# A mixture of 32 experts, half of them narrowed to 64 rows and multiplied in plain float32 on two column halves of TensorE

## The reference

```
grp   = argmax(x @ w_group + b_group)                    # one of 4 groups per token
e1,e2 = top-2 of the 8 experts of that group
y     = w1 * expert(e1, x) + w2 * expert(e2, x)
expert(e, x) = (silu(x @ w_gate[e]) * (x @ w_up[e])) @ w_down[e]
```

## Time and profile before

| | |
|---|---|
| median of three runs | 1117.98 us |
| the profiled execution: own time, span | 1120.31 us, 1118.5 us |
| expert stage, first transpose of rows to the first instruction after down of the last | 497.2 to 1072.3 us |
| TensorE busy, share of the span | 98% |
| VectorE, ScalarE | 71%, 56% |
| moved by DMA | 288.3 MB |

### The profile page before, as it was taken

How to read it: one execution, slowest core, us unless ns; L and a number is a source line. 1 busy time by engine, 2 the same in 40 slices (tenths; PEclk the granted TensorE clock), 3 DMA queues, 4 the chain that set the end, 5 groups by cost and what they waited for, 6 DMA issues and landing times.

```text
span 1118.5 us, 15317 instructions
## 1 busy us (share of the span) xinstructions
PE 1090.7 (98%) x5369; PEld 901.1 (81%) x5369; DVE 799.0 (71%) x1127; ACT 626.6 (56%) x698; POOL 206.0 (18%) x187
## 2 busy tenths in 40 slices
PE   8999999999999999989999999999999999999976
PEld 7778899688887787868888888888888888888842
DVE  4220521245648787789999999998898989889787
ACT  5322231224336210247888887788888788888644
POOL 3001112000000000012343322233232332423200
PEclk9999999999999999989999999999999999999998
DMA  8622314811123321169999999999999999999784
GB/s 303 227 71 80 123 51 128 270 33 65 38 78 113 123 92 69 57 252 394 395 363 381 389 389 377 396 386 383 387 373 389 378 390 373 385 397 384 284 346 197
DMA packets 73369, 288.32 MB, mean 258 GB/s; under 512 B 16229, under 2 KB 24549, under 8 KB 47716
## 3 DMA queue, kind: packets, MB, share of 16 engines
q1 hardware_dynamic: 60320, 258.34, 60.8%
q0 software_dynamic: 11840, 25.09, 5.8%
q10 hardware_dynamic: 1156, 4.20, 0.9%
HBM read 266.66 MB, written 37.75 MB: 272 GB/s over the span
## 4 chain that ended last, share of the span: by engine, by line
PE 93%; DVE 3%; DMA 2%; issue 1%; ACT 1%; DVEq 0%; POOL 0%; POOLq 0%; ACTq 0%
PE bank L1651 26%; PE bank L1653 26%; PE bank L1652 26%; PE bank L1999 3%; PE bank L2099 2%; PE bank L2034 1%; PE bank L1837 1%; PE bank L1839 1%; PE bank L1886 1%; PE bank L1842 1%; DMA expert_rows<-yt,dix 1%; PE bank L1851 1%; PE bank L1797 1%; PE bank L1878 1%; PE bank L1729 1%
## 5 line engine op out<-in xcount | busy, mean ns | idle before, releaser
L1651 PE MATMUL bank<-whi,xghi 128*128 128x512 f32 x512 | 203.3, 397 | 1.0 <-DVE xglo L1495 1.0
L1653 PE MATMUL bank<-whi,xglo 128*128 128x512 f32 x512 | 200.4, 391 | 0.0
L1652 PE MATMUL bank<-wlo,xghi 128*128 128x512 f32 x512 | 199.9, 391 | 0.0
L1482 DVE TENSOR_TENSOR wlo<-raw_down,whi 128x2048 fp32r<-128x2048 f32 x64 | 146.2, 2292 | 27.8 <-ACT whi L825 27.7
L1651 PE MATMUL bank<-whi,xhi 128*128 128x512 f32 x384 | 155.2, 404 | 0.9 <-ACT num L768 0.6
L1653 PE MATMUL bank<-whi,xlo 128*128 128x512 f32 x384 | 151.3, 394 | 0.0
L1652 PE MATMUL bank<-wlo,xhi 128*128 128x512 f32 x384 | 151.0, 393 | 0.0
L1482 DVE TENSOR_TENSOR wlo<-raw,whi 128x2048 fp32r<-128x2048 f32 x64 | 146.4, 2288 | 4.2 <-ACT whi L825 3.2
L1482 DVE TENSOR_TENSOR wlo<-raw_up,whi 128x2048 fp32r<-128x2048 f32 x64 | 146.3, 2287 | 0.0
L825 ACT ACTIVATE whi<-raw_up 128x2048 fp32r<-128x2048 f32 x64 | 122.4, 1914 | 25.7 <-PE bank L1653 25.3
L825 ACT ACTIVATE whi<-raw_down 128x2048 fp32r<-128x2048 f32 x64 | 122.4, 1913 | 23.7 <-PE bank L1653 23.7
(11 more groups left out here) (341 smaller groups left out, 1708.9 us busy)
## 6 DMA issues: line engine op xcount, KB each, us to landing
raw<-l_w_gate SPq DMA_DIRECT2D x64, 1024.0 KB, 8.3
raw_up<-l_w_up SPq DMA_DIRECT2D x64, 1024.0 KB, 8.4
raw_down<-l_w_down SPq DMA_DIRECT2D x64, 1024.0 KB, 8.7
raw<-l_w_in SPq DMA_DIRECT2D x5, 2048.0 KB, 9.3
yy<-expert_rows SPq DMA_DIRECT2D x8, 1024.0 KB, 8.1
xt<-x_cols SPq DMA_DIRECT2D x8, 512.0 KB, 4.8
o_rows<-stage POOLq DMA_DIRECT2D x16, 256.0 KB, 3.2
qkT<-qk_rows SPq DMA_DIRECT2D x16, 256.0 KB, 3.7
```

The costliest lines, as they stand in the source:

```text
L1482: tt(wlo[k][:, halves(p)], raw_e[k][:, halves(p)], whi[k][:, halves(p)].bitcast(F32), ALU.subtract).then_inc(e_lo[k], 1)
L1651: t.matmul(out, lh, rh, start=first, stop=False)
L1652: t.matmul(out, lh, rl, start=False, stop=False)
L1653: return t.matmul(out, ll, rh, start=False, stop=last)
```

## The change

Experts are no longer taken in the order of their numbers. Experts 0 and 1 come first, as two with 128 rows ("large"). VectorE sorts the other 30 by their number of rows (`order`); the fifteen with most rows are large too, the other fifteen take 64 rows ("small"). Then come 15 pairs of one small and one large expert, and down of the last large one.

A small expert has its own buffers for weights, rows, hidden values and results. Its weights are used as loaded, with no `hi` and `lo`. Each chunk is two plain float32 matmuls with 64 stationary columns. One writes partitions 0 to 63 of bank 7 and the other 64 to 127: up and gate, or the two halves of down. That makes 16 matmuls for gate and up, 8 for down, and 12 transposes of 64 rows.

A large expert keeps its 72 matmuls and its 12 transposes. The low part of its weights is now written over the loaded weights, so a half of `raw_b` is free for its next load only when the matmuls on it are done. There is one `xghi` and `xglo` instead of two. An expert with more rows than its 64 or 128 would get a further pair; with these inputs there is none.

Further: some semaphores are merged (`wg_raw`, the gate biases, `hnw` and the meta tokens share one that waits for all four). The routing pieces move to pairs 1 to 5. The residual rows of all tiles are loaded before the last expert's end, where half of them were loaded after it.

The order on each engine in the expert stage:

```diff
@@ TensorE
+        def gate_up_small(s, p):
+            if p == 0:
+                pe.wait_ge(N["xs_cp"], s + 1)
+                wait(pe, N["y_s_cp"], s * 2)
+            wg, wu = [raw_s[k][:].rearrange("p (k n) -> p k n", k=KC) for k in range(2)]
+            pe.wait_ge(small_landed[0][p], s * 32 + 64)
+            for kk in range(4 * p, 4 * p + 4):
+                t.matmul(ps[7][0:SMALL, :], xT_s[:, kk, :], wu[:, kk, :], start=kk == 0, stop=kk == KC - 1)
+                last = t.matmul(ps[7][SMALL:, :], xT_s[:, kk, :], wg[:, kk, :], start=kk == 0, stop=kk == KC - 1)
+            last.then_inc(N["gu_s_mm"], 1)
...
+        def down_large(n, q):
+            pe.wait_ge(N["g_lo"], n + 1)
...
+                if q == 0 and k % 2 == 0:
+                    pe.wait_ge(e_lo[2], n * 2 + (k // 2 + 1))
...
+        def pair(i, ahead=1):
...
+            gate_up_small(i - 1, 0)
+            hidden_large(i)
+            gate_up_small(i - 1, 1)
...
+            rows_large(i + 1)
+            down_large(i, 0)
+            hidden_small(i - 1)
+            down_large(i, 1)
+            gate_large(i + 1)
...
+            down_small(i - 1)
             if ahead:
...
+                rows_small(i)
+            up_large(i + 1)
...
+        rows_large(0)
+        gate_large(0)
+        up_large(0)
+        rows_large(1)
+        hidden_large(0)
+        gate_large(1)
+        down_large(0, 0)
+        down_large(0, 1)
+        rows_small(0)
+        up_large(1)
@@ ScalarE
+        def pair(i, ahead=1):
+            silu_large(i)
+            hidden_hi(i)
+            hi_large(i, 2, 0)
+            silu_small(i - 1)
+            xg_hi(i + 1)
+            hi_large(i, 2, 1)
+            hi_large(i + 1, 0, 0)
+            hidden_small(i - 1)
+            y_large(i, 0)
+            hi_large(i + 1, 0, 1)
+            y_large(i, 1)
+            hi_large(i + 1, 1, 0)
+            y_small(i - 1)
             if ahead:
...
+                x_small(i)
+            hi_large(i + 1, 1, 1)
@@ VectorE
+        xg_lo(0)
+        order()
+        lo_large(0, 1, 1)
         for p in range(2):
...
+            lo_large(0, 2, p)
+        lo_large(1, 0, 0)
+        times_up(0)
+        lo_large(1, 0, 1)
+        xg_lo(1)
+        hidden_lo(0)
...
+        def pair(i):
+            times_up(i)
+            hidden_lo(i)
...
+            lo_large(i, 2, 0)
+            times_up_small(i - 1)
+            xg_lo(i + 1)
+            lo_large(i, 2, 1)
+            lo_large(i + 1, 0, 0)
...
+            lo_large(i + 1, 0, 1)
...
+            lo_large(i + 1, 1, 0)
+            lo_large(i + 1, 1, 1)
@@ SP, loads
+        def load_pair(i):
+            small = expert_at(i * 2)
+            for p in range(2):
+                for k in range(2):
+                    load_small(i - 1, small, k, p)
...
+                down_of(i)
+            large = expert_at(i * 2 + 1)
+            load_large(i + 1, large, 0)
+            for p in range(2):
+                load_small(i - 1, small, 2, p)
+            load_large(i + 1, large, 1)
```

More of the change, by code:

```diff
@@ L478, in _ @@
[L478 to L488, removed]
@@ L496, in _ @@
+        sp.wait_ge(N["ordered"], 1)
+        for i in range(1, 4):
+            load_pair(i)
+        sp.wait_ge(N["routed_n"], 1)
+        last_pair = sp.value_load(npm1[0:1, 0:1], min_val=PAIRS - 3, max_val=PAIRS - 3 + EXTRA) + 2
+        with sp.Fori(4, last_pair) as i:
+            load_pair(i)
+        load_pair(last_pair)
+        down_of(last_pair + 1)
+        sp.wait_ge(N["gu_s_mm"], last_pair * 2)
         for n in range(EARLY):
@@ L608, in scatter @@
[L608 to L616, removed]
@@ L619, in _, with gather_large @@
-        STATIC = 12
-        for s in range(2):
-            pool.sem_inc(tix_ready[s], STATIC + 2)
+        def gather_large(n, column=None):
+            wait(pool, N["xgT_mm"], n * 2)
+            if isinstance(n, int) and n < FIRST:
+                rows = tokrow[:, n:n + 1]
+            else:
+                if isinstance(n, int) and n == FIRST:
+                    g.memset(xg_b[:], 0.0)
+                rows = tix_b[:]
+                pool.wait_ge(gathered_b, n * 16)
+                g.tensor_copy(rows, tokrow[:, bass.ds(column, 1)]).then_inc(tix_b_ready, 1)
+                pool.wait_ge(tix_b_ready, n - (FIRST - 1))
+                pool.sem_inc(N["wait_passed"], 1)
+            g.indirect_dma_start(xg_b[:], None, h1_dram[0:T, :], bass.IndirectOffsetOnAxis(rows.bitcast(U32), 0),
+                                 bounds_check=last_token, oob_is_err=False).then_inc(gathered_b, 16)
@@ L827, in xg_hi, with hi_large @@
-        def xg_hi(j, b):
+        def hi_large(n, k, p):
+            if isinstance(n, int) and n == 1:
+                act.wait_ge(small_landed[k // 2][p], (32, 16)[k // 2])
+                act.wait_ge((N["g_mm"], N["u2_mm"], N["y2_mm"])[k], (p + 1, p + 1, p + 2)[k])
+                src = raw_s[k]
+            else:
+                act.wait_ge(ex_landed[k][p], 16 if isinstance(n, int) and n == 0 else n * 16)
+                src = raw_b[k]
+            a.activation(whi[k][:, halves(p)], src[:, halves(p)], ACT.Copy).then_inc(e_hi[k], 1)
@@ L852, in _, with y_small @@
+        def y_small(s):
+            wait(act, scattered_s, s * 16)
+            act.wait_ge(N["y_s_mm"], s * 2 + 2)
+            for q in range(2):
+                a.activation(yt_s[:, q * 512:(q + 1) * 512], ps[7][q * SMALL:(q + 1) * SMALL, :], ACT.Copy).then_inc(N["y_s_cp"], 1)
         for i in range(NT - 1):
@@ L869, in _ @@
         a.activation(r_s[:, 1, :], r_s[:, 0, :], ACT.Exp).then_inc(N["w_exp"], 1)
-        xg_hi(0, 0)
+        xg_hi(0)
         a.activation(ftmp[:, 0:1], ones[:, 0:1], ACT.Silu)
-        hi_expert(0, 2, 1)
-        hi_expert(1, 0, 0)
-        xg_hi(1, 1)
-        hi_expert(1, 0, 1)
-        silu(0)
+        hi_large(0, 2, 1)
+        hi_large(1, 0, 0)
+        silu_large(0)
+        hi_large(1, 0, 1)
+        xg_hi(1)
+        hidden_hi(0)
+        hi_large(1, 1, 0)
+        hi_large(1, 1, 1)
+        y_large(0, 0)
+        y_large(0, 1)
+        x_small(0)
         def scale_rows(tiles):
@@ new lines, in _ @@
+        for i in range(1, 4):
+            pair(i)
+        act.wait_ge(N["routed_n"], 1)
+        last_pair = act.value_load(npm1[0:1, 0:1], min_val=PAIRS - 3, max_val=PAIRS - 3 + EXTRA) + 2
+        with act.Fori(4, last_pair) as i:
+            pair(i)
+        pair(last_pair, ahead=0)
+        last = last_pair + 1
+        silu_large(last)
+        hi_large(last, 2, 0)
+        hidden_hi(last)
+        hi_large(last, 2, 1)
+        scale_rows((0, 1, 2))
+        a.activation(diags[:, 0, :], ident[:], ACT.Copy, scale=ALPHA).then_inc(N["f_scaled"], 1)
@@ L927, in squares @@
+        weight_diagonals((4,))
+        y_large(last, 0)
+        scale_rows((3,))
+        y_large(last, 1)
         def squares(n):
@@ L1566, in expert_sum @@
+        for i in range(1, STATIC):
+            pair(i)
+        dve.wait_ge(N["routed_n"], 1)
+        last_pair = dve.value_load(npm1[0:1, 0:1], min_val=PAIRS - 3, max_val=PAIRS - 3 + EXTRA) + 2
+        with dve.Fori(STATIC, last_pair) as i:
+            pair(i)
+        pair(last_pair)
+        last = last_pair + 1
+        times_up(last)
+        lo_large(last, 2, 0)
+        hidden_lo(last)
+        lo_large(last, 2, 1)
+        last_tokens(last)
         def expert_sum(n):
@@ L2051, in item @@
[L2051 to L2067 removed]
+            wl = lo_b[2][:].rearrange("p (k n) -> p k n", k=FC)
@@ new lines, in hidden_small, with down_small @@
+        def hidden_small(s):
+            pe.wait_ge(N["gu_s_done"], s + 1)
+            pe.sem_inc(N["wait_passed"], 1)
+            gv = gu_s[:].rearrange("p (m k) -> p k m", k=FC)
+            for k in range(FC):
+                last = t.transpose(ps[4][:, k * SMALL:(k + 1) * SMALL], gv[:, k, :], ident[0:SMALL, 0:SMALL])
+            last.then_inc(N["hT_s_mm"], 1)
+        def down_small(s):
+            pe.wait_ge(N["hT_s_cp"], s + 1)
+            wd = raw_s[2][:].rearrange("p (k n) -> p k n", k=FC)
+            for k in range(FC):
+                if k % 2 == 0:
+                    pe.wait_ge(small_landed[1][k // 2], s * 16 + 32)
+                t.matmul(ps[7][0:SMALL, :], hT_s[:, k, :], wd[:, k, 0:512], start=k == 0, stop=k == FC - 1)
+                last = t.matmul(ps[7][SMALL:, :], hT_s[:, k, :], wd[:, k, 512:], start=k == 0, stop=k == FC - 1)
+                if k % 2:
+                    last.then_inc(N["y_s_mm"], 1)
```

704 lines of the change are left out of this document (378 added, 326 removed).

## The result

The changed kernel takes 1210.32 us (median of 4 runs, 1207.23 to 1212.96), the kernel before 1117.31 in the same comparison: 1.0826 times as long, 95% interval 1.0802 to 1.0851. That is 93 us slower, where the forecast was 1173 (56 slower, range 1075 to 1215). The direction and the range held. The size did not: 37 us are missing from the sum, and the time lies above the 1145 to 1200 that the prediction gave as its likeliest rival's own range. The profiled execution took 1212.96 us, its span 1211.2.

The account below looks back on a forecast made before the run. TensorE bounds, with loads at 92% of their limit. Start 38.6, fifteen pairs of 38.7, routing 3 and end 8.7 make 630.8 us against 575.1, 55.7 more: 1173 us, range 1075 to 1215.

Parts of the forecast that it names:

- its likeliest rival: Small experts' matmuls on both column halves run together, with waits in each pair: 1173 us, own range 1145 to 1200, chance 0.67.
- the routing: Routing pieces moved to pairs 1 to 5, where VectorE is part of the chain: 0 to 8 us, taken as 3.
- the end: From the end of the last up, the last expert's hidden and down take 8.7 us, as before.
- Work of a pair: TensorE's work in a pair: 17.8 large expert, 10.3 small expert's matmuls, 1.2 its transposes; 29.3 us.
- Waits: TensorE's idle time in a pair, for copies and low parts on the other engines: 7.7 us together.
- Down's 4.4: Wait in the large expert's down: its second half's high part stands on ScalarE behind the next rows' copy; 4.4 us.
- up's 2.9: Wait in the next large expert's up: its second half's high part stands behind the small expert's copies; 2.9 us.
- gate's 0.4: Wait in gate of a pair: its second half comes 0.4 us late behind the copy of a large expert's result.
- The clock: TensorE's half-clock stretches after a pair's two waits: up to 3.4 us of work lost, taken as 1.7.
- the partial rival: The column halves overlap only partly, a small expert's matmuls cost 13 us: 40 more, 1213 us, chance 0.05.
- One after the other: The column halves don't overlap, a small expert costs 20.6 us and a pair 49.0: 154 more, 1328 us, chance 0.15.
- Loads become the bound: Faster rival: ScalarE and VectorE run ahead, so loads set the pair at 32.7 us: 1084 us, chance 0.13.

Follow-up runs that it names:

- the run with fewer bytes: The reordered kernel, reading only an eighth of each half of the small experts' down weights: 1056.3 us.
- the two runs that change one order each: Changed kernel with down's high and low parts made earlier: 1115.0 us; changed kernel with the high part of up's second half copied earlier: 1157.7 us.
- The smallest edit: Changed kernel with down's wait for a result copy-out made smaller by one, to the same half of the expert before: 1175.0 us.
- The filled waits: Changed kernel with order and waits kept, but TensorE multiplying the identity by itself into a free bank while it waits: 1163.3 us.
- the run on one half: Changed kernel with small experts' gate and up, and down's two halves, on the same column half, into two different banks: 1352.1 us.
- the reordered kernel: Changed kernel with the weaker copy-out wait, down's parts earlier (also for the last expert) and up's second half earlier: 1095.5 us.

## Why the prediction held, and by which terms it was too small

**The sum.** Measured on the same marks as in the forecast, the start of the stage took 537.05 - 497.43 = 39.6 us (forecast 38.6), the pairs 1158.2 - 537.05 = 621.2 (580.5 and 3 for the routing), the end 1170.18 - 1158.2 = 12.0 (8.7). From there to the end of the span it is 41.0, against 46.2 before: the tail gained 5.2 where I took 0. Off by 1.0, 37.7, 3.3 and -5.2, together the missing 37. Nearly all is the pair: 41.2 instead of 38.7, fifteen times. Of these 2.5 us, 1.7 are work, 1.4 are clock, and the waits took 0.7 off: two terms too small and one too large.

**Work of a pair.** Forecast 29.3, measured 31.0 by the run with fewer bytes: 25 us in fifteen pairs, the largest miss of the sum. The choice that the halves run together was right: a two takes 0.86. The yield of 1.59 that I estimated from the Trainium skill (TensorE: Matmul & The Clock Gate, Part 3) would have been 13.0 us for a small expert's matmuls; three blocks of 3.59 are 10.8, against 20.6 one by one. What was mis-sized are the transposes and the changes from one kind of instruction to another, about 0.1 each. The large expert's four transposes took 0.39 from start to start before (728.95 to 729.34) and take 0.68 now in front of plain float32 matmuls. In the pair of 31.00 us the small blocks took 10.75 where the sum held 10.3, the large expert's 72 matmuls 17.0 for 16.6, and the transposes 3.2 (0.68 and 0.90 for the large expert's, 0.62 and 1.03 for the small one's, from start to start) for 2.4.

**Waits.** Forecast 7.7, measured 6.4 idle and about 0.6 at their edges: the last matmul before a wait runs 0.40 where its slot is 0.23, and the first one behind it takes 0.33. Down's 4.4 was 3.2, up's 2.9 was 2.2, and gate's 0.4 did not come. Their places and their causes were as said, and the two runs that change one order each show it. For one wait the sum has no term at all: 1.05 before down's second half. `y_cp >= 2n + 1` is the copy-out of the first half of the same expert, and that copy stands on ScalarE behind `hidden_small`. The smallest edit removes it.

**The clock.** I took 1.7 a pair, half of the 3.4 that two full slow stretches could cost, because part of a stretch might lie in the wait. The filled waits put it at 3.1, 21 us more in fifteen pairs. In the pair shown both stretches come after the wait, in working time.

**The start, the routing, the end.** The first three pairs took 42.2 (from 540.64 three of them to 667.37) and the next eleven 41.3 (to 1121.73), so the routing cost about 3, as taken. The end was 3.3 longer: the last expert's down waits three times as well (0.94, 1.19 and 0.78).

**Where the range held by luck.** The period of a pair, 41.2, is outside the 37 to 40 that the prediction named as the sign of its mechanism, and the time is outside that mechanism's own 1145 to 1200. The outer range reached 1215 only because of the partial rival, and the time comes within 3 us of that rival's 1213 by other terms: the small expert took 10.8 and not 13.

**The rivals.** *One after the other* is excluded by the twos in the trace, and its price, 154 more, was close: 142 in the run on one half. *Partly together* fell too, by the blocks of 3.59, though its number was the nearest of all. *Loads become the bound* needed waits and clock to shrink to 5.7 together; they were 7.0 + 3.1 = 10.1. For the changed kernel it was wrong, since ScalarE doesn't run ahead. What it said of the loads holds in another kernel: with the orders changed they do bound, at 33.5 us a pair against my 32.7, and the time was 1095.5 against 1084. The Trainium skill's 358 GB/s for a core (DMA: Bandwidth & Descriptors, Specifications) is no limit here, on one core: the reordered kernel moved 418 over 80 us.

**Where the gain went.** The change takes 35.6 - 31.0 = 4.6 us of TensorE's work out of each pair, and gives back 7.0 in waits and 3.1 in clock. The cover was lost: before, each low part had 24 matmuls of another weight in front of it. Now down's and up's second halves have six and twelve. The small expert's matmuls need no parts and could be that cover, but they stand elsewhere.

## What to carry to other kernels

When an edit makes the bounding engine's work shorter, walk through the in-order queues of the others again: copies that were free may stand behind something that waits for the bounding engine. Here waits of 1 to 3 us on TensorE cost nearly half as much again through its clock (3.1 beside 7.0 a pair), so removing one of several waits can bring more than its length, and the cheap test is to fill the wait with useless matmuls. Two plain float32 matmuls of 64 stationary columns on the two column halves cost as much as one, 0.86 us.

## What the runs showed of the hardware

The first instruction on the second column half started beside the fifth of eight that stand before it in the program, on the first half. The Trainium skill (TensorE: Matmul & The Clock Gate, Part 3) says that matmuls are strictly in order in start and end; the starts in the trace of the run with one half issued after the other do not agree (807.45 for a later one, 807.87 for an earlier one).

In the run with the weaker wait, two neighbouring pairs with the same two waits were granted 1.00 and 0.88 of the clock: the same wait is not always followed by a slow stretch. Why is open.

One core's loads ran at 418 GB/s over 80 us and at 399 over 480 us, where the kernel before reached 384.
